# A hybrid mixer and mixture-of-experts step on one core: the instructions around the router put in another order

## What is computed

```python
h = layer_norm(x) * (1 + sc1) + sh1              # sh1, sc1, g1, sh2, sc2, g2 = silu(cond) @ w_ada + b_ada
u = h @ w_in                                     # three mixers: gated scan, Fourier, short convolution
merged = sum(gate_b * (branch_b @ w_proj_b))
x = layer_norm(ALPHA * x + g1 * (merged @ w_out), ln1_g, ln1_b)
h = layer_norm(x) * (1 + sc2) + sh2
scores = sigmoid(h @ w_router)                   # 64 experts, each token takes the top 8
routed = sum over the token's experts of gate * (silu(h @ w_gate[e]) * (h @ w_up[e])) @ w_down[e]
shared = (silu(h @ w_sh_gate) * (h @ w_sh_up)) @ w_sh_down
y = layer_norm(ALPHA * x + g2 * (routed + shared), ln2_g, ln2_b)
```

## Time and profile before

| | us |
|---|---|
| median of the runs | 960.85 |
| the profiled execution's own time | 961.3 |
| its span, first to last instruction | 958.7 |
| TensorE busy / VectorE / ScalarE / GpSimd | 842.7 / 399.5 / 177.0 / 63.9 |
| HBM read | 283.85 MB |

### The profile page before, as it was taken

How to read it: one execution, slowest core, us unless ns; L and a number is a source line. 1 busy time by engine, 2 the same in 40 slices (tenths; PEclk the granted TensorE clock), 3 DMA queues, 4 the chain that set the end, 5 groups by cost and what they waited for, 6 DMA issues and landing times.

```text
span 958.7 us, 14199 instructions
## 1 busy us (share of the span) xinstructions
PE 842.7 (88%) x5634; PEld 506.9 (53%) x5634; DVE 399.5 (42%) x943; ACT 177.0 (18%) x304; POOL 63.9 (7%) x62
## 2 busy tenths in 40 slices
PE   1799969988899998789999979898998989899991
PEld 0387458444455444776555545454554545455550
DVE  2120576766553517632333424334233424234336
ACT  1212331111112211221111111111111111111221
POOL 0000124234410000000000000000000000000000
PEclk8799979999999999589999989999999989999996
DMA  8963322556575086547999999999999999999931
GB/s 288 381 203 129 135 87 88 187 189 235 202 273 201 32 300 256 202 176 300 416 416 415 416 416 418 416 416 416 417 415 418 416 417 416 417 415 416 417 129 44
DMA packets 77328, 286.37 MB, mean 299 GB/s; under 512 B 9008, under 2 KB 11056, under 8 KB 60112
## 3 DMA queue, kind: packets, MB, share of 16 engines
q1 hardware_dynamic: 73200, 276.72, 73.2%
q0 software_dynamic: 2144, 5.84, 1.9%
q10 hardware_dynamic: 1920, 2.92, 0.9%
HBM read 283.85 MB, written 1.61 MB: 298 GB/s over the span
## 4 chain that ended last, share of the span: by engine, by line
PE 71%; DMA 11%; DVE 9%; issue 4%; ACT 2%; POOL 1%; PEldq 0%; SPq 0%; ACTq 0%; PEld 0%; DVEq 0%
PE bank L1753 20%; PE bank L1794 10%; PE bank L1495 7%; PE bank L1779 6%; DMA ring<-in_w_exp_up 6%; PE bank L1740 6%; PE bank L1502 4%; DMA ring<-in_w_ada 3%; PE bank L1621 3%; PE bank L1636 2%; PE bank L1766 2%; DVE lev_e L1088 2%; PE bank L1518 2%; PE bank L1475 2%; PE bank L1647 1%
## 5 line engine op out<-in xcount | busy, mean ns | idle before, releaser
L1753 PE MATMUL bank<-ring,x_g 128*64 128x256 f32 (+1 forms) x1760 | 180.6, 401 | 22.3 <-issue 12.4
L1753 PEld LDWEIGHTS bank<-ring,x_g 128*64 128x64 f32 (+1 forms) x1760 | 106.7, 131 | 100.9 <-issue 58.8
L1502 PE MATMUL bank<-ring,h_t 128*128 128x512 f32 x256 | 112.9, 594 | 2.0 <-issue 2.0
L1794 PE MATMUL bank<-down_w,hid_t 128*64 128x512 f32 (+1 forms) x592 | 112.1, 602 | 0.0
L1379 DVE COPY hid_t<-bank 128x128 f32<-128x128 f32 x58 | 16.9, 291 | 189.1 <-PE bank L1768 189.1
L1403 DVE TENSOR_TENSOR y_lo<-bank,y_hi 128x512 fp32r<-128x512 f32 x58 | 40.1, 692 | 113.4 <-ACT y_hi L923 113.4
L1502 PEld LDWEIGHTS bank<-ring,h_t 128*128 128x128 f32 x256 | 47.5, 190 | 61.7 <-issue 61.7
L1753 PE MATMUL bank<-up_more,x_g 128*64 128x256 f32 (+1 forms) x608 | 72.7, 394 | 5.5 <-DMA ring<-in_w_exp_up 5.1
L1495 PE MATMUL bank<-h_t,ring 128*128 128x256 f32 x288 | 66.2, 392 | 2.3 <-DVE h_t L1019 1.8
L1495 PEld LDWEIGHTS bank<-h_t,ring 128*128 128x128 f32 x288 | 56.3, 197 | 11.4 <-issue 3.4
L923 ACT ACTIVATE y_hi<-bank 128x512 fp32r<-128x512 f32 x58 | 34.6, 597 | 138.2 <-PE bank L1794 138.2
(11 more groups left out here) (247 smaller groups left out, 896.3 us busy)
## 6 DMA issues: line engine op xcount, KB each, us to landing
down_w<-in_w_exp_down SPq DMA_DIRECT2D x66, 1024.0 KB, 16.0
ring<-in_w_exp_gate SPq DMA_DIRECT2D x49, 1024.0 KB, 14.5
ring<-in_w_exp_up SPq DMA_DIRECT2D x49, 1024.0 KB, 17.4
ring<-in_w_in SPq DMA_DIRECT2D x13, 2048.0 KB, 8.8
ring<-in_w_ada SPq DMA_DIRECT2D x12, 2048.0 KB, 9.5
up_more<-in_w_exp_gate SPq DMA_DIRECT2D x17, 1024.0 KB, 14.4
up_more<-in_w_exp_up SPq DMA_DIRECT2D x17, 1024.0 KB, 17.0
ring<-in_w_out SPq DMA_DIRECT2D x2, 2048.0 KB, 10.7
```

The costliest lines, as they stand in the source:

```text
L1502: ins = mm(out[:, :], h_t[:, k, tok(h)], w[:, k, :], start=k == 0, stop=k == KD - 1)
L1753: ins = mm(gu_bank[at:at + rows, 0:2 * P].rearrange("p (b n) -> p b n", b=2), x[:, k, i * rows:(i + 1) * rows], up_w[slot][:, :, k, h * P: ...
L1794: ins = mm(y_bank[at:at + rows, :], hid_t[:, f * SLOTS + i * rows:f * SLOTS + (i + 1) * rows], down_w[:, slot, f, h * BANK:(h + 1) * BANK] ...
```

## The change

The listed work and its loads stand in another order; the mathematics is the same.

1. Unit order "AA" + "ABCBA" * 8 in place of "BCBAA" * 8 + "AA". Still 54 units and 62 loads.
2. Output projection by group (both halves for group 0, then group 1). Both `out` chunks are released together at the end.
3. Residual, norms: group 0's two residuals, its norms, then group 1's.
4. Router weights (`w_rt`, `b_rt`) are loaded from ScalarE's queue at the scan's final states, not after the mixers.
5. TensorE after the projection: turn group 0, the two last modulations (banks 6 and 7), logits of group 0, `shared_up` of both f for group 0, turn group 1, its logits, `shared_up(0, 1)`, place and count, `shared_up(1, 1)`, rows, then the four gathers, `halves`, `half_rows`, and unit 0.
6. `shared_down` moves into unit 1. Its weights have their own tile `w_sh_d` and are no chunk any more, so loads 1, 2 and 3 take the slots of `ada` 10, `ada` 11 and `shared_up`. SP issues `w_sh_d` ahead of load 3.
7. The list moves into units 2 to 5 on VectorE, and ahead of up(3), up(4), up(5) on TensorE.
8. The last two modulation rows (VectorE) move into unit 0; ScalarE waits for their store in unit 1 and loads the ln2 rows there.
9. ScalarE copies `h_t` first and makes the high part `h_hi` after it.

```diff
-    for kind in "BCBAA" * 8 + "AA":
+    for kind in "AA" + "ABCBA" * 8:
...
-          + [("shared_up", 0), ("shared_down", 0)])
+          + [("shared_up", 0)])
...
+                    if load == RING:
+                        sp.wait_ge(*read_out(("h2", 1, 1)))
+                        sp.wait_ge(h_lo_ready, G)
+                        sp.dma_start(w_sh_d[:, :, :], tiles(w_sh_down[0])).then_inc(sh_down_in, 16)
...
+                    act.dma_start(w_rt[:, :, :], rows8(w_router[0])).then_inc(router_in, 16)
+                    act.dma_start(b_rt[:, :], row(b_router[0])).then_inc(router_in, 16)
...
+                if n == 1:
+                    for s in mod_stored:
+                        act.wait_ge(s, 16 * len(ADA_ROWS) // 2)
+                    act.dma_start(ln2_rows[0][:, :], row(ln2_g[0])).then_inc(ln2_in, 16)
+                    act.dma_start(ln2_rows[1][:, :], row(ln2_b[0])).then_inc(ln2_in, 16)
...
             two_norms(0)
-            residual(1, 1)
+            for h in range(2):
+                residual(h, 1)
             nc.vector.drain().then_inc(mixer_done, 1)
             two_norms(1)
-            for n in range(late, len(ADA_ROWS)):
-                modulation_row(n)
...
-                hidden(n)
+                hidden(n, {LIST_AT: take_before, LIST_AT + 1: take_items, LIST_AT + 2: take_item_rows}.get(n))
                 w_picks_of(n + 1)
                 put_backs(n, n % 2)
+                if n == 0:
+                    for r in range(late, len(ADA_ROWS)):
+                        modulation_row(r)
+                if n == LIST_AT - 1:
+                    count_chunks()
+                if n == LIST_AT:
+                    list_items()
...
-            for h in range(2):
-                w = arrived(("out", h)).rearrange("p (k n) -> p k n", k=KD)
-                for g in range(G):
+            for g in range(G):
+                for h in range(2):
+                    w = arrived(("out", h)).rearrange("p (k n) -> p k n", k=KD)
...
-                nc.tensor.drain().then_inc(chunk_used, 1)
+            nc.tensor.drain().then_inc(chunk_used, 2)
             nc.tensor.drain().then_inc(mixer_done, 1)
...
+            turn_h2(0)
+            for c in ADA_LAST:
+                modulation(c)
+            for a in range(2):
+                pe.wait_ge(*read_out(("h2", 0, a)))
+            pe.wait_ge(a_ready, 1)
+            pe.wait_ge(router_in, 32)
+            logits(0)
+            for f in range(2):
+                shared_up(f, 0)
+            turn_h2(1)
+            for a in range(2):
+                pe.wait_ge(*read_out(("h2", 1, a)))
+            logits(1)
+            shared_up(0, 1)
...
+                if n == 1:
+                    pe.wait_ge(*read_out(("half_rows",)))
+                    shared_down()
```

More of the change, by code:

```diff
@@ L199 @@
             + [("proj", g, h, b) for g in range(G) for h in range(2) for b in BRANCH_ORDER]
-            + [("out", h, g) for h in range(2) for g in range(G)]
+            + [("out", h, g) for g in range(G) for h in range(2)]
             + [("ada", c) for c in ADA_LAST]
@@ L250 @@
            + [("h2", g, a) for g in range(G) for a in range(2)]
-           + [("logits",), ("place",), ("count",), ("rows",), ("halves",), ("half_rows",), ("before",), ("items",), ("item_rows",)])
+           + [("logits",), ("place",), ("count",), ("rows",), ("halves",), ("half_rows",)])
 SCRATCH_NO = {u: n for n, u in enumerate(SCRATCH)}
@@ L475, in hybrid_layer @@
         silu_sh_ready = sem("silu_sh_ready")
+        last_rows_out, shared_out = sem("last_rows_out"), sem("shared_out")
+        sh_down_in = sem("sh_down_in")
         dve_step, act_step = sem("dve_step"), sem("act_step")
         def evacuated(product):
+            kind, c = product[0:2]
+            if kind == "shared":
+                return shared_out, c + 1
+            if kind == "ada" and c in ADA_LAST:
+                return last_rows_out, ADA_LAST.index(c) + 1
             n = PRODUCT_NO[product]
@@ L487, in rotating @@
         def rotating(product):
-            if product == ("shared", 1):
-                return bank[7]
+            kind, c = product[0:2]
+            if kind == "shared":
+                return bank[1 + c]
+            if kind == "ada" and c in ADA_LAST:
+                return bank[6 + ADA_LAST.index(c)]
             return product_bank[PRODUCT_NO[product] % N_ROT]
         def scratch(use):
-            if use == ("logits",):
+            if use in (("logits",), ("count",), ("halves",)):
                 return o_bank[0]
+            if use in (("place",), ("rows",), ("half_rows",)):
+                return y_bank
             return scratch_bank[SCRATCH_NO[use] % 2]
@@ L515, in gather_from @@
         def gather_from(j, a):
-            return bank[1 + a % 2] if j == 0 else gather_bank
+            return bank[0] if j == 0 and a % 2 else gather_bank
         def loads_of(n, q=None):
@@ L1370, in _, with count_chunks @@
-            taken(("item_rows",), nc.vector.tensor_copy(item_weight[:, :, :], two[:, 1]))
-            for f in range(2):
-                hidden_shared(f)
+            hidden_shared(1)
+            def count_chunks():
+                step(nc.vector.tensor_scalar(below[:, :], con("cap_from")[mine, :], rank[:, 0:1], None, ALU.is_gt))
+                step(nc.vector.scalar_tensor_tensor(cap[:, :], below[:, 0:1], 2.0, below[:, 1:2], ALU.mult, ALU.add))
+                step(nc.vector.scalar_tensor_tensor(cap[:, :], below[:, 2:3], -1.0, cap[:, :], ALU.mult, ALU.add))
+                step(nc.vector.tensor_scalar(cap[:, :], cap[:, :], float(HALF), float(SLOTS), ALU.mult, ALU.add))
+                nc.vector.tensor_scalar(chunk_from[:, :], con("chunk_at")[mine, :], cap[:, 0:1], None, ALU.add)
+                step(nc.vector.tensor_tensor(over[:, :], counts[:, :], cap[:, :], ALU.subtract))
+                step(nc.vector.tensor_scalar(has_chunk[:, :], con("chunk_at")[mine, :], over[:, 0:1], None, ALU.is_lt))
+                nc.vector.reduce_sum(n_chunks[:, :], has_chunk[:, :], axis=AXX).then_inc(counted, 1)
@@ L1453, in bank_for @@
                 n = PRODUCT_NO[product]
-                if n >= N_ROT:
+                if product[0] == "shared":
+                    pe.wait_ge(*evacuated(("out", 1 - product[1], product[1])))
+                elif n >= N_ROT and product[1] not in ADA_LAST:
                     pe.wait_ge(bank_free[n % N_ROT], n // N_ROT)
@@ L1686, in _ @@
             ins.then_inc(scratch_ready, 1)
-            shared_up(1, 0)
-            pe.wait_ge(*read_out(("count",)))
-            out = scratch_for(("halves",))
-            mm(out[0:1, 0:len(HALVES)], con("part_no")[0:N_EXP, :], of_half[:, :], start=True, stop=True).then_inc(scratch_ready, 1)
-            pe.wait_ge(*read_out(("rows",)))
-            out = scratch_for(("half_rows",))
-            for a in range(2):
-                for g in range(G):
-                    i = (a * G + g) * len(HALVES)
-                    ins = mm(out[:, i:i + len(HALVES)], rows_t[:, a, g, :], of_half[:, :], start=True, stop=True)
@@ L1697, in _ @@
-            ins.then_inc(scratch_ready, 1)
-            shared_up(1, 1)
-            nc.tensor.drain().then_inc(chunk_used, 1)
-            pe.wait_ge(counted, 1)
-            out = scratch_for(("before",))
-            mm(out[0:N_EXP, 0:1], before[0:N_EXP, 0:N_EXP], n_chunks[:, :], start=True, stop=True)
-            mm(out[0:1, 1:2], n_chunks[:, :], ones[0:N_EXP, 0:1], start=True, stop=True).then_inc(scratch_ready, 1)
-            for g in range(G):
-                pe.wait_ge(a_ready, g + 1)
@@ L1707, in _ @@
-            w = arrived(("shared_down", 0))[:, 0:2 * D].rearrange("p (k n) -> p k n", k=2)
-            def shared_down(g):
-                for h in range(2):
-                    for f in range(2):
-                        ins = mm(acc_bank[2 * g + h][:, :], hid_sh[:, f, tok(g)], w[:, f, h * BANK:(h + 1) * BANK], start=f == 0, stop=f == 1)
-            pe.wait_ge(listed, MORE_CHUNKS)
-            out = scratch_for(("items",))
-            mm(out[0:1, 0:MAX_ITEMS], con("part_no")[0:N_EXP, :], of_item[:, :], start=True, stop=True)
@@ L1717, in _, with shared_down @@
-            mm(out[:, P:P + MAX_ITEMS], ones[0:N_EXP, :], at_item[:, :], start=True, stop=True).then_inc(scratch_ready, 1)
-            out = scratch_for(("item_rows",))
-            for a in range(2):
-                for g in range(G):
-                    i = (a * G + g) * MAX_ITEMS
-                    ins = mm(out[:, i:i + MAX_ITEMS], rows_t[:, a, g, :], of_item[:, :], start=True, stop=True)
-            ins.then_inc(scratch_ready, 1)
+            def shared_down():
+                pe.wait_ge(sh_down_in, 16)
+                pe.wait_ge(*evacuated(("shared", 1)))
+                pe.wait_ge(*evacuated(("ada", ADA_LAST[-1])))
+                pe.wait_ge(*read_out(("halves",)))
+                pe.wait_ge(x_ready, ITEMS_PER_TURN)
+                for g in range(G):
+                    for h in range(2):
```

(9 more changed lines are left out.)

143 lines of the change are left out of this document (73 added, 70 removed).

## The result

The changed kernel takes 952.26 us (median of four runs, 949.71 to 955.18) against 960.5 for the kernel before on the same chip: a ratio of 0.9919, interval 0.9897 to 0.9942, 0.8% faster. The forecast was 948.3. The profiled execution took 955.18, with a span of 952.2.

A forecast was written before the change was run, and what follows sets the result against it. The weight stream at 416 GB/s was taken to bound the experts' stretch. Terms 423.8 + 420.9 + 101.0 = 945.7 against a span of 958.7, 13.0 less, so 961.3 - 13.0 = 948.3 us; 8-in-10 range 938 to 958.

The forecast's parts named there:

- way to up(0): From the output projection's start to the end of unit 0's up product: 82.4 us, ending at 423.8, 16.8 sooner.
- wait for `ada` 11: TensorE, ahead of the second modulation, stands 4.2 us for this chunk, which lands at 380.3.
- second rival: Clock stays at its lower level through the router: up(0) at 435, time 959, no change to be told; chance 0.13.
- stretch behind up(0): From the end of up(0) to the last weight wait, at unit 49: 420.9 us, against 393.25 before.
- costed at nothing: List, modulation rows and `count_chunks` on VectorE in units 0 to 5: about 12 us of small work, taken as hidden.
- One sign of being right: Weight stream at 416 GB/s from about 20 us after up(0).
- gap of unit 1: `shared_down` in unit 1 holds back the next loads to 15.1 after up(0), past 12.6 of queued work: 2.5 us.
- the 2.1 MB: The g2 and ln2 rows now pass within the weight stream: 5.0 us at its rate, taken as 6.
- tail: From the last weight wait, at unit 49, to the end of the span: 101.0 us against 124.8, 23.8 less.
- order of units: New unit order by itself: 27.6 us more before the last weight wait, 23.8 less after, so 3.8 go back.
- first rival: Clock returns at once and the 2.1 MB fill gaps: up(0) at 417.3, 414.9 remain, time 936; chance 0.18.
- third rival: Queue runs dry behind seven single-expert units at the stream's head, making the kernel slower, 966; chance 0.09.

The follow-up runs named there:

- both edits: Changed kernel with the overflow list in units 26 to 28 and the last two modulation rows ahead of VectorE's wait for `halves`: 945.15 us, ratio 0.9839.
- traffic late: Changed kernel with the loads of the g2 and ln2 rows held back to unit 52: 954.86 us, ratio 0.9935 to the kernel before.
- rows early: Changed kernel with the last two modulation rows made ahead of VectorE's wait for `halves`, not in unit 0: 949.06 us, ratio 0.9890.
- list late: Changed kernel with the overflow list made in units 26 to 28 in place of 3 to 5: 946.71 us, ratio 0.9874.
- all four: Changed kernel with late list, projection by column half, modulation rows and `hidden_shared(1)` ahead of VectorE's wait for `halves`: 933.13 us, ratio 0.9713.
- projection by halves: Changed kernel with the output projection by column half again (product order, chunk release, residuals): 947.44 us, ratio 0.9870 to the kernel before.

## Why the prediction was nearly right, point by point

**The way to up(0)** was right in mechanism and near in its sum: 82.4 from the start of the output projection forecast, 80.3 measured. That it came so near is partly luck, since three sizes inside it were off and cancelled. The wait for `ada` 11 was 5.39 for 4.2 and ended 41.0 behind the start of the projection, not 38.9: the second to fourth `out` products took 22.56 for three times 7.0, and the transfer landed in 8.6, not 7.8. The clock was at 0.50 under the modulation, as I took it. But it was back at 1.00 by 388: the first logits took 2.02 where I had them up to 387.8 at 3.7, and everything up to the gathers went at full clock. Logits of group 1 ended at 400.5, not 402.9, and from `ada` 11 to the end of the gathers it was 30.6 for 36.5. The second rival (a clock that stays low to 415) fell with that. From the gathers to up(0) it was 3.4, as forecast, though I had not said that TensorE stands still for 1.97 of it; up(0) at 5.36 behind that stop gives back 1.7.

**The stretch behind up(0)** is the term that was mis-sized: 420.9 forecast, 426.6 measured. The step that failed is what the prediction costed at nothing: list, modulation rows and `count_chunks`. I named the condition (a first wait on VectorE in units 0 to 5), but for unit 0 I took `shared_down` as the cover. It was none: it waited for the rows itself, since `shared_down` first waits until VectorE has read the bank of `ada` 11. The some 2 us that I named for a cover that is gone were the right size. For the list I argued from VectorE's mean load, 18.39 of 54 us. That mean says nothing of a chain of instructions that one unit needs, and the list held unit 4 for 2.14, with a product at the lower clock after it. Both together cost 426.6 - 419.2 = 7.4, by the kernel without them (list alone 4.2, rows alone 2.5). One sign of being right failed with it: the stream was not at 416 GB/s from about 20 us after up(0) on, but at 219 from 460 to 465.

Two more sizes inside the term were wrong and cancelled: the gap of unit 1 and the 2.1 MB. I had SP's next issue at 15.1 behind up(0), but in that sum I took off a product of 3.67, up(2), that has to pass first. With both edits the issues of units 0 and 2 are 18.6 apart (421.59 and 440.22 in SP's queue); less the 12.6 of queued work that is a gap of 6.0 in place of 2.5. The 2.1 MB, 5.0 at the stream's rate, fit into it, and my 6 for them was not there: traffic late has the gap without the bytes and the same stretch. With 412.4 for the weights and their latency, as forecast, the budget is then, in the changed kernel, 412.4 + 8.0 (20.55 from 423.05 to 443.60, less 12.6) + 6.4 (the late units) = 426.8 for 426.6 measured; with both edits 412.4 + 6.0 = 418.4 for 419.2. For rows early alone it gives 423.1 (a gap of 6.0, late units 4.7) against 424.1. For list late alone it gives 420.3 against 422.4, so some 2 us there stay unexplained.

**The tail** was 1.8 longer than 101.0: the two-expert unit behind the last wait took 6.53 in this execution, against 5.08; it is 4.92 in the kernel with all four.

**The sum.** -0.95 in the end of up(0) (its way 2.1 shorter, its start 1.1 later), 5.7 in the stretch and 1.8 in the tail make 6.5 in the span, and the profiled execution is 6.9 over the forecast. It was the slowest of four; the median is 4.0 over.

**The order of units** was worth 3.8 us against, by the forecast; measured, it can't be told from nothing either way, in three pairs. The 3.8 was misread: it holds other parts of the change, above all the 2.5 of the gap and the 6 of the rows. Three loads more against a tail 23.8 shorter is 22.8 - 23.8, a gain of 1.0; the order alone in the kernel before gave 22.5 and 23.6. **The first rival** came half true: the clock was back early and the 2.1 MB filled gaps. But its 414.9 for the stretch left out what list, rows and the larger gap cost.

**The third rival**, a queue that runs dry, was half seen: the engines were busy for only 0.17 and 0.54 of their time around 422 and 462. But what was late was TensorE's release of the slots: with list and rows moved, the same loads issued in the same way have it at 1.00 from 425 on.

**The clock.** The Trainium skill (TensorE: Matmul & The Clock Gate, "Part 1: The HAM clock gate") has the throttled clock as the default and activity as what releases it. The trace agrees with the direction: the products at the lower level shown above stand behind a stop. The trace doesn't tell which stop will cost: up(0) took 5.36 behind a stop of 1.97 in the changed kernel and 3.67 behind the same 1.97 in the kernel with both edits.

## What to carry to other kernels

Work that is moved beside a pipeline's first units is not hidden by an engine's mean load: ask which instruction of that very unit stands behind it, and whether the work that is named as its cover uses the same banks. Where loads are released by the end of each unit, a stop in the opening is for the most part paid (7.4 us, where units ran 6.4 late for the list and unit 1 stretched the gap by 2.0), and the same stop some twenty units later left the stream as it was. And a term that comes out right as a sum should be looked through for two errors that cancel.

## What the runs showed that was not expected

The lower clock after a short stop is not the same from run to run. After 1.97 idle, up(0) took 5.36 in six profiles and 3.67 in one; after 2.13 of idle up(4) took 5.36 in the kernel with the projection by halves and 3.67 in the kernel with early rows. How long it stays low differs too: behind the wait for `ada` 11 the first logits took 2.02 in the changed kernel and 3.65 in the kernel with list and rows moved, after 5.39 and 5.76 of idle, but 1.97 after 5.96 in the kernel with the late list. The second to fourth `out` products, one row of the timeline, are another case: they took 22.56 behind stops of 2.48 to 2.73, and 20.87 behind 1.90 and 2.24, so there the longer stops were the costly ones. A cost of 1.7 us per stop of about 2 us is thus a possible, not a sure one; a forecast should give it a chance and not count it as certain.
